# Seven block products in place of eight in column tiles 9 to 15 of an input projection, on one Trainium2 core

## The reference, cut to what matters

```
xn = rmsnorm(x, g_pre)            # (2112, 1024)
u = xn @ w_in                     # (2112, 10240) and 16 low-rank columns
gq, gk, gv, gg, glr, dq, dk, dv, dg, ga, gb = split(u)
```

## Time and profile before

| what | value |
|---|---|
| median of 3 runs | 2802.56 us (2802.45 to 2804.43) |
| the profiled execution: span | 2799.7 us |
| span plus what lies around it | 2802.6 us, taking the median for its own time |
| TensorE busy | 2769.4 us, 99% |
| VectorE, ScalarE, GpSimd busy | 38%, 31%, 13% |
| mean granted TensorE clock | 0.998 of full speed |
| projection | the first 2153 us of the span |

### The profile page before, as it was taken

The page is one execution under the profiler, slowest core; times in us unless marked ns, Lnnn a source line. Parts: engine busy times, 40 slices in busy tenths (PEclk is TensorE's granted clock), DMA queues, the critical chain, the costliest instruction groups (busy, mean ns, idle before and its releaser), DMA issues.

```text
span 2799.7 us, 40580 instructions
## 1 busy us (share of the span) xinstructions
PE 2769.4 (99%) x16108; PEld 1453.6 (52%) x16108; DVE 1077.3 (38%) x2401; ACT 861.5 (31%) x1728; POOL 360.3 (13%) x601
## 2 busy tenths in 40 slices
PE   8999999999999999999999999999999899999998
PEld 4444456555545665666555555555544344444444
DVE  6211134444333443344223333333322655555452
ACT  5111124444312222333123321111112544444441
POOL 2000011111311002120011113222100000000000
PEclk9999999999999999999999999999999999999999
DMA  9543464655577566584576789787646966556642
GB/s 283 134 168 132 147 208 152 214 177 207 190 253 286 187 195 213 185 273 152 179 278 208 257 234 301 239 249 252 216 152 224 277 172 174 148 149 180 164 112 58
DMA packets 326542, 558.35 MB, mean 199 GB/s; under 512 B 179114, under 2 KB 184305, under 8 KB 321874
## 3 DMA queue, kind: packets, MB, share of 16 engines
q1 hardware_dynamic: 268722, 290.57, 34.9%
q0 software_dynamic: 43376, 231.63, 25.3%
q10 hardware_dynamic: 14256, 33.56, 3.3%
HBM read 378.70 MB, written 236.79 MB: 220 GB/s over the span
## 4 chain that ended last, share of the span: by engine, by line
PE 96%; DMA 1%; SPq 1%; DVE 1%; ACT 0%; issue 0%; POOL 0%; DVEq 0%; POOLq 0%
PE out L2654 40%; PE out L2214 22%; PE out L2651 18%; PE out L1143 2%; PE out L1128 2%; PE out L2657 2%; PE out L1134 1%; PE out L615 1%; PE out L626 1%; PE out L625 1%; PE out L1429 1%; PE out L1389 1%; DMA mix_pe_in<-in_p_prompt 1%; SPq L356 1%; PE out L1117 1%; PE out L1402 0%
## 5 line engine op out<-in xcount | busy, mean ns | idle before, releaser
L2654 PE MATMUL out<-w_hi,xn_hi 128*128 128x512 f16 x1792 | 679.9, 379 | 1.0 <-DVE w_lo L2514 0.5
L2654 PE MATMUL out<-w_lo,xn_hi 128*128 128x512 f16 x1792 | 679.4, 379 | 0.0
L2654 PE MATMUL out<-w_hi,xn_lo 128*128 128x512 f16 x1792 | 679.4, 379 | 0.0
L2545 ACT ACTIVATE stage<-out 128x512 f32<-128x512 f32 (+1 forms) x170 | 99.4, 585 | 926.9 <-PE out L2654 613.2
L2592 DVE TENSOR_SCALAR stage<-out 128x512 f32<-128x512 f32 (+1 forms) x170 | 114.7, 675 | 645.0 <-PE out L2654 398.4
L2651 PE MATMUL out<-xn_hi,w_hi 128*128 128x512 f16 x768 | 291.3, 379 | 0.0
L2651 PE MATMUL out<-xn_hi,w_lo 128*128 128x512 f16 x768 | 291.1, 379 | 0.0
L2651 PE MATMUL out<-xn_lo,w_hi 128*128 128x512 f16 x768 | 291.1, 379 | 0.0
L2654 PEld LDWEIGHTS out<-w_hi,xn_lo 128*128 128x128 f16 x1792 | 175.4, 98 | 211.5 <-issue 0.3
L2654 PEld LDWEIGHTS out<-w_hi,xn_hi 128*128 128x128 f16 x1792 | 175.8, 98 | 192.6 <-issue 6.2
L2654 PEld LDWEIGHTS out<-w_lo,xn_hi 128*128 128x128 f16 x1792 | 175.4, 98 | 186.4 <-issue 0.3
(11 more groups left out here) (320 smaller groups left out, 3950.5 us busy)
## 6 DMA issues: line engine op xcount, KB each, us to landing
out<-in_cache_kv_w POOLq DMA_DIRECT2D x64, 1020.0 KB, 9.8
U<-stage SPq DMA_DIRECT2D x224, 256.0 KB, 4.6
raw<-in_w_in SPq DMA_DIRECT2D x78, 512.0 KB, 5.1
UT<-stage SPq DMA_DIRECT2D x96, 256.0 KB, 4.2
sw_kc<-in_cache_kv_w ACTq DMA_DIRECT2D x24, 1024.0 KB, 9.6
sw_vc<-in_cache_kv_w POOLq DMA_DIRECT2D x24, 1024.0 KB, 9.4
sw_rows<-U POOLq DMA_DIRECT2D x32, 512.0 KB, 7.8
out<-in_cache_kv_w POOLq DMA_DIRECT2D x16, 1008.0 KB, 8.0
```

Source lines behind the costliest of these rows:

```text
L2545: move_out(act, m, lambda o, x: act.activation(o, x, ACT.Copy, scale=1.0 / W_SCALE))
L2654: last = pe.matmul(out[m % 3][:, :], x[:, k, at:at + P], y[:, k, :], start=first, stop=final)
```

## The change

In column tiles 9 to 15 (slots 306 to 543) the projection works on pairs of token tiles. A pair's product, [two token tiles] x [two halves of k] by [two halves of k] x [two halves of the columns], is made of seven block products by the Strassen-Winograd scheme. Each block product is 4 steps of k times 3, so 12 products of 128 x 128 by 128 x 256. Eight pairs with seven products and one unit for the samples make 57 units, spread over the 34 slots. Four of the seven left factors are sums of blocks of xn, made once by VectorE in slots 58 to 129, stored to DRAM (`X`) and loaded again for every pair of every one of the seven tiles, 2 x 512 KB a pair, into the place of half of xn's odd token tiles; what lay there is kept in `KEPT` and brought back at the end. Four of the seven right factors are sums of blocks of weights, made by GpSimd once per tile. Seven hi halves are cut by ScalarE and seven lo halves by VectorE during a tile's last pair, into a ring of 8. A pair's results leave PSUM in seven pieces, two by ScalarE and five by VectorE, which adds them up in the stage buffers. `Windows` has one buffer for keys and one for values in place of two, loaded in four parts each. The order of the column tiles 7 to 12, three start slots and the release of semaphores change as well. The low half of the file (waits counted over the tiles that are not changed) is left out.

```
-WINDOW_SLOTS = [277, 351, 452]
-SAMPLE_SLOT, SAMPLE_PERIOD = 527, 15
+WINDOW_SLOTS = [277, 385, 449]
+SAMPLE_SLOT, SAMPLE_PERIOD = 524, 15
+MADE_BY = [7, 11, 13]
+SEVEN_FIRST, SEVEN_LAST = 9, 15
+W_RING, W_SHIFT = 8, 4
+SUM_SLOT, SUM_PERIOD = 58, 9
...
+    SUM = {1: 1, 2: 0, 4: 2, 5: 3}
+    SCALAR = {0: 1, 3: 2}
+    VECTOR = {1: 1, 2: 2, 4: 3, 5: 4, 6: 5}
+    def product_bank(self, j, pair, i):
+        a, b, c = self.roles[j * PAIRS + pair]
+        return (a, b, c, a, b, c, b)[i]
+    def wait_bank(self, pe, j, pair, i, staged):
...
+        elif i == 3:
+            pe.wait_ge(self.scalar_kept, self.scalar_at(j, pair, 0))
+        else:
+            pe.wait_ge(self.vector_kept, self.vector_at(j, pair, {4: 1, 5: 2, 6: 4}[i]))
+    def tensor(self, pe, n, slot, staged):
+        j = n - SEVEN_FIRST
+        for unit in units_at(slot):
...
+            self.wait_bank(pe, j, pair, i, staged)
+            if pair == 0:
+                pe.wait_ge(self.op_lo, j * PRODUCTS + i + 1)
+            if i == 1:
+                pe.wait_ge(self.sums_loaded[pair % 2], 32 * ((j * PAIRS + pair) // 2 + 1))
+            for k in range(HALF_K):
+                for order, (x, y) in enumerate(((0, 0), (0, 1), (1, 0))):
+                    last = pe.matmul(bank[:, :HALF], self.left(j, pair, i, x, k), self.right(j, i, y)[:, k, :],
+                                     start=i < 3 and k == 0 and order == 0, stop=k == HALF_K - 1 and order == 2, skip_group_check=True)
...
+    def scalar(self, act, n, slot):
...
+                if pair == PAIRS - 1 and i < PRODUCTS - 1:
+                    act.wait_ge(self.made, self.made_at(j, unit))
+                    self.cut_hi(act, j + 1, i + 1)
+    def add_blocks(self, pool, j, step):
...
+        if step == 3:
+            pool.wait_ge(self.op_lo, j * PRODUCTS + 1)
+            pool.wait_ge(self.block_added, 4 * j + 2)
+            pool.tensor_tensor(b11, b21, t2, ALU.subtract).then_inc(self.block_added, 1)
+    def vector(self, dve, n, slot):
...
+                dve.scalar_tensor_tensor(out=part, in0=bank[:, :HALF], scalar=1.0 / W_SCALE, in1=lower[:, :HALF] if i < 3 else part,
+                                         op0=ALU.mult, op1=ALU.add).then_inc(self.vector_kept, 1)
+            if j + 1 < SEVENS:
+                if (pair, i) == (PAIRS - 2, 6):
+                    self.cut_lo(dve, j + 1, 0)
+                if pair == PAIRS - 1 and i > 0:
+                    self.cut_lo(dve, j + 1, i)
+    def load_sums(self, sp, j, pair):
+        r = pair % 2
+        for part in range(2):
+            sp.dma_start(self.xn[part][:, 1, 4 * r:4 * r + 4, :HALF_K, :], self.X[part, pair]) \
+              .then_inc(self.sums_loaded[r], 16)
+    def queue(self, sp, n, slot, U, column):
...
+            if i == 5:
+                x = j * PAIRS + pair + 2
+                sp.wait_ge(self.made, self.made_at(j, unit))
+                if x < SEVENS * PAIRS:
+                    self.load_sums(sp, *divmod(x, PAIRS))
...
+            for c in range(self.PARTS):
+                if r == at + 6 + c * self.PART:
+                    self.load_k(q, g, h, c)
+                if r == at + 12 + c * self.PART:
+                    self.load_v(q, g, h, c)
...
+                if n == SEVEN_LAST and q % TILE_SLOTS == 8:
+                    sevens.cut_done(sp)
+                    for i in range(RAW):
+                        load_raw(sp, piece_of(n + 1, i))
+                if n == SEVEN_LAST + 1 and q % TILE_SLOTS in (0, 1):
+                    for i in range(RAW):
+                        load_raw(sp, piece_of(n, RAW * (1 + q % TILE_SLOTS) + i))
...
+                    if n == SEVEN_LAST and q % TILE_SLOTS == TILE_SLOTS - 1:
+                        for i in range(RAW):
+                            cut_lo_piece(dve, piece_of(n + 1, i))
+                    if n == SEVEN_LAST + 1 and q % TILE_SLOTS == 0:
+                        for i in range(RAW, PIECES):
+                            cut_lo_piece(dve, piece_of(n, i))
```

More of the change, by code:

```diff
@@ L190, with seven, sample_place, plain_tiles @@
 CUT_SLOT, CUT_PERIOD = 170, 10
+SEVEN_FIRST, SEVEN_LAST = 9, 15
+SEVENS = SEVEN_LAST - SEVEN_FIRST + 1
+HALF_K = K_TILES // 2
+HALF = BANK // 2
+PAIRS = SEQ // (2 * P)
+PRODUCTS = 7
+UNITS = PAIRS * PRODUCTS + 1
+SAMPLE_UNIT = PAIRS // 2 * PRODUCTS
+W_RING, W_SHIFT = 8, 4
+SUM_SLOT, SUM_PERIOD = 58, 9
+def seven(n):
+    return SEVEN_FIRST <= n <= SEVEN_LAST
+def sample_place(n):
+    return PAIRS if seven(n) else TOKEN_TILES - 1
+def plain_tiles(n):
+    return sum(not seven(i) for i in range(n))
+def plain_before(m):
+    n, place = divmod(m, TOKEN_TILES)
+    return sum((i * TOKEN_TILES + t) % 2 == m % 2 for i in range(n + 1) if not seven(i) for t in range(TOKEN_TILES)
+               if i < n or t < place)
+def plain_made(m):
+    return plain_before(m) + 1
+def pair_of(unit):
+    return divmod(unit if unit < SAMPLE_UNIT else unit - 1, PRODUCTS)
+def unit_slot(unit):
+    return unit * TILE_SLOTS // UNITS
+def units_at(slot):
+    return [u for u in range(UNITS) if unit_slot(u) == slot]
+def pair_place(pair):
+    return 2 * pair if pair < PAIRS // 2 else 2 * pair + 1
 def wait(eng, sem, n):
@@ L416, in landed @@
     def landed(self, e, s, tiles):
-        return 16 * sum(2 if m % TOKEN_TILES == TOKEN_TILES - 1 else 1 for m in range(tiles) if m % 2 == e and m // 2 % 2 == s)
+        return 16 * sum(2 if m % TOKEN_TILES == sample_place(m // TOKEN_TILES) else 1 for m in range(tiles) if m % 2 == e and m // 2 % 2 == s)
     def wait_tiles(self, eng, tiles):
@@ L2303, in later, with later_load @@
             return Later(signal, base)
+        def later_load(name):
+            signal, base = next(left_loads, None) or (sem(name, start=0), 0)
+            return Later(signal, base)
         with ExitStack() as region:
-            samples = Samples((core.bind(region)[0], sem, later), side, U, caches, a["sample_mask"], identity, OG)
+            top = core.bind(region)[0]
+            top("sw_low", [P, (SIDE_BYTES - BLOCK_BYTES) // 4])
+            late = top("sw_new_k", [P, WIDTH]), top("sw_new_v", [P, WIDTH]), \
+                [top(f"sw_rows{s}", [P, Samples.PAIR, WIDTH]) for s in range(Samples.RING)]
+        with ExitStack() as region:
+            samples = Samples((core.bind(region)[0], later, later_load), late, side, U, caches, a["sample_mask"], identity, OG)
         with ExitStack() as region:
@@ L2364, in side_queue @@
                 q.wait_ge(empty_stored, 16)
+                sums.done(q)
             if slot == GLA_SLOT - 3:
```

754 lines of the change are left out of this document (591 added, 163 removed).

## The result

| | kernel before | changed kernel |
|---|---|---|
| median of the runs | 2802.51 us | 2856.8 us (2853.86 to 2860.26) |
| ratio to before | | 1.0192, 95% interval 1.0179 to 1.0204 |
| span of the profiled execution | 2799.7 us | 2852.1 us (whole time 2853.86) |

The change made the kernel slower by 54 us. I had forecast 2784 us, with a range of 2750 to 2822, and a chance of 0.30 for slower. The measured time is outside the range.

The account below looks back on a forecast made before the run. TensorE's stream of products, busy 99% of the span, was taken as the bound. 2799.7 - 65.8 + 13 + 11 + 18 + 5 = 2780.9 us of span, plus 2.9 around it, gave 2784 us; range 2750 to 2822.

Parts of the forecast that it names:

- What the products give: Column tiles 9 to 15: half-wide products 0.109 us apart save 9.4 us a tile, 65.8 us over seven tiles.
- The rival with the weight loads: New products: each pair of load and product takes 0.120 us, so 52 us come back, 2836 us; chance 0.04.
- VectorE at the crossings: Last pair at six tile crossings: VectorE's lo cuts make TensorE wait, 13 us; ends 0 if run-ahead absorbs it, and 21.
- Tile 15 to 16: Start of tile 16: TensorE waits 2.2 us for cuts and 8.5 for pieces 2 and 3, together 11 us; ends 2.2, 21.
- The DMA queues: Tiles 14 and 15: the added sums loads overfill the queues, 18 us for all transfers; ends 0 and 28.
- rival on starving: Projection pairs: waits for sums replace the saved products, 50 us with the tiles beside, 2818 us; slower side, chance 0.26.
- one values part: Tile 14: a window's values, issued at slot 477 behind 8 MB of `keep_rows`, make TensorE wait 0 to 20 us.
- The clock: After idle stretches of TensorE the clock halves, 1.5 us lost each; three such stretches, 5 us; ends 0 and 9.
- Nearly all kept: Transfers slide and TensorE's run-ahead absorbs the crossings: 3 + 7 + 0 + 2 returned, 2749 us; chance 0.12.
- GpSimd and VectorE: Tile crossings: GpSimd's add blocks a lo cut, 7 us over six by rows (2791 us), 13.5 by skill (2798); chance 0.05.

Follow-up runs that it names:

- no_sum_loads: Changed kernel without loading the sums of xn from the third pair on, nor waiting for them (54 pairs reuse the first two): 2767.9 us, ratio 0.9873.
- tile16_early: On top of shifts_outside, pieces 2 and 3 of tile 16's weights are loaded during tile 15 into ring places no longer read: 2791.7 us, ratio 0.9960.
- before_shifts_outside: Control: the kernel before, with the cache shift copies of column tiles 9 to 16 issued in tiles 1 to 8 and 17 to 19: 2802.75 us, ratio 0.9998.
- shifts_outside: Changed kernel with the 1 MB cache shift copies of tiles 9 to 15 issued in tiles 1 to 8 and 17 to 19: 2796.6 us, ratio 0.9979.

## Why the prediction was wrong

**What the products give** was nearly right. New products lie 0.109 us apart, with 128 columns of weights loaded for each. Where little waits, as in no_sum_loads, the stretch of tiles 9 to 15 is 732 us. Less 19.0 us of waits and 6.2 for the lower clock, that leaves 707, and in the changed kernel the same sum leaves 710, against 767 - 66 = 701 by the forecast. Where the 6 to 9 us went I did not trace. The rival with the weight loads falls.

**VectorE at the crossings**, 13 us, was too much. The rows that can be VectorE's are masks (2.0 us) and its own pieces (1.4 us), 3.4 in all, and 0.3 of that follows a late store. I had summed VectorE's and TensorE's work over one pair. Why it is hidden was not tried; the run-ahead of the window steps, which was my lower end, is a guess.

**Tile 15 to 16** was right in its sum: 11 us forecast, 10.0 measured. The parts were 2.2 and 8.5 and came as 3.3 and 6.7, so two errors partly cancel. tile16_early shows that the second was the transfer.

**The DMA queues** is the step that failed: "I take **18 us** for all transfers", "ends 0 and 28". Sums and stores cost 49.4 + 31.3 = 80.7 us. Three things were wrong with it. First, I held the demand against the ceiling in tiles 14 and 15 alone and costed the other five at nothing, since they read a share of 0.5 to 0.7. The first wait, of 7.4 us, is in tile 9, whose share before was 0.58. A mean over a tile says nothing of a burst, and a load with a lead of 12 to 18 us sees only the burst. Held over the whole stretch the sum would have warned: 170 + 59 MB in 701 us is 327 GB/s, just under the 339 which I had read as the most that lasts. Second, I wrote that the stores "have four stage buffers of room" and priced them at nothing. A pair fills two of the four, and its lower buffer, stored after product 6, is wanted again after product 0 of the pair after next: eight products later, one less than the sums have. The stores that TensorE ended up waiting for took 6 to 23 us to land. What waits for them is ScalarE, 140.6 us in 16 places, and the windows' keys stand behind it. Third, the rival on starving gives the sums "a lead of two pairs". They are issued behind product 5 of one pair and needed at product 1 of the pair after next, which is nine products or 1.3 pairs; at 12.1 us a pair that is 15.6 us and not 24.

The one values part that I had priced behind `keep_rows`, 0 to 20 us, made no wait here; in no_sum_loads, where TensorE comes there earlier, it made one of 4.8.

**The clock**, 5 us with ends 0 and 9, failed with it: twelve stretches in tiles 9 to 15 and two at tile 16 in place of three, and 28.0 us. The mechanism was as described; the count followed the waits.

The sum with the measured terms: 2799.7 - 65.8 + 3.4 + 10.0 + 82.1 + 28.0 = 2857.4. Before the mix stage the wait of 8.6 us is gone, which makes 2848.8. The span is 2852.1, so 3 us are not assigned; with the 6 to 9 us that the products gave less, it is 3 to 6 too many. Why the 8.6 us are gone was not looked into. The longest wait of the kernel before was another, 10.4 us ahead of the first product; it is 9.1 now and changes nothing.

**The rivals.** The one on the slower side, the sums starve, had the mechanism and the sign. Its 50 us for the sums met the 49.4 measured, which is partly luck, as it had most of them in tile 14 and they lie in all seven tiles. It left out the stores and nearly all of the clock. Its argument against itself, "the copies of caches can slide", was the mistake: they don't slide by themselves. They are issued at fixed slots and take their share of the engines there. Once moved by hand they gave 60 us, and before_shifts_outside shows that this is worth nothing without the change. Nearly all kept falls. No single transfer is the cause: with the bytes of the sums gone the time is 2768, with the shift copies elsewhere 2797, and with the sums issued earlier, or (on top of shifts_outside) the weight block in smaller parts, it stays where it was. Not tried: more stage buffers, the stores on another queue or ahead of the sums, and ScalarE's piece behind its key copy. Two window buffers in place of one were not tried either, but no wait of TensorE in these runs ends with a load of keys.

**GpSimd and VectorE.** An add holds up a lo cut, but the price is small. The cut of 128x1024 is 1.21 us elsewhere; beside GpSimd's last add in tile 10, in the timelines of GpSimd and VectorE, it was

```profile
1161.84 2.36 POOL L777 TENSOR_TENSOR w_block<-w_block,w_sum 128x1024 f32<-128x1024 f32 x1 [17.89 <-DVE w_ring2l L758]
```

```profile
1162.82 0.42 DVE L809 SCALAR_TENSOR_TENSOR stage<-out,stage 128x256 f32<-128x256 f32 x1 [1.06 <-PE out L703]
1163.16 2.12 DVE L758 SCALAR_TENSOR_TENSOR w_ring3l<-w_sum,w_ring3h 128x1024 f16<-128x1024 f32 x1
```

The two overlap by 1.04 us and the cut is 0.90 longer. Three others (tiles 12, 13 and 14) overlap by 0.38 and are 0.25 longer. That fits, within 0.14 us, the rule in the Trainium skill, "SBUF — State Buffer", section "Who interferes with whom", that the second of the two is blocked while the first runs. The piece at L809, with one operand in PSUM, kept its 0.42 us beside the same add. The adds' means are 2.36 to 2.42 us, and the prediction's estimate was 2.25. Over six crossings it is some 1.7 us and not the 7 or 13.5 weighed, since the adds are mostly done before the cuts begin.

## What to carry to other kernels

When products become cheaper and need more bytes, divide all the bytes of the stretch by its new length before anything else, and list the bursts in it with the lead of each load that sits inside. Transfers with no deadline (cache copies, kept results) should first be moved out of the stretch, to a place whose own deadlines on the same queue have been looked up: both of my first two places for `keep_rows` made a wait of 13 to 25 us. A wait that goes away when its load is issued earlier, while the time stays, says that something behind it on the queue is as late; here fewer bytes in that stretch helped, and an earlier issue did not. And where the releaser in a wait is an engine that works in order, ask what that engine itself was waiting for: a row that named a copy of keys was a store of results.

## What I had not expected of the hardware

A 1 MB copy from DRAM to DRAM cost nothing in a stretch with a mean of 222 GB/s and 1.5 us each in one with 283 GB/s; no run lies between. A load of 512 KB took as little as 4.2 us to land in quiet places and 20 to 30 in the burst around 1540 us, issued by the same line. In that burst one queue had 81.4% of the engines and the other 19.6%, with transfers of 20 us and more open in both. And four loads of 512 KB in place of one of 2 MB, spread over nine slots, left the landing of the sums as it was, 20.0 against 20.6 us (two of the four were issued ahead of these sums).
